# Swapping the rows for the turning by position with small transfers, in a fused float32 kernel on one Trainium2 core

## The chip, the core and the metric

The program runs on one core of a Trainium2 chip. The core has five engines that run side by side, each in its own written order, and that wait for each other through semaphores: TensorE (PE in the profile; its weight loads are shown as PEld), VectorE (DVE), ScalarE (ACT), GpSimd (POOL) and SyncE (SP, which here only issues transfers). The metric is the device time of one execution in microseconds, and less is better. The kernel before takes 1328.01 us, the median of three runs (1327.96 to 1329.7).

## The reference, cut to what matters

Two transformer blocks are computed in float32 for 256 tokens of width 1024. The change lies in the first of them, in what follows its wide input projection `w_in`:

```python
proj = xn @ w_in                       # (256, 1024) @ (1024, 4680)
u_pool, q, k, v, iq, ik, iw, gates = split(proj)
q, k, iq, ik = rope_partial(each)      # the turning by position

def rope_partial(x, pos):              # heads of 64; only the first 16 of each turn
    xr = x[..., :16]; x1, x2 = xr[..., :8], xr[..., 8:]
    rot = concatenate([x1 * cos - x2 * sin, x2 * cos + x1 * sin])
    return concatenate([rot, x[..., 16:]])

score = sum over 8 index heads of  iw * relu(iq @ ik / 8)   # then the 64 largest of a row
p     = softmax of q @ k / 8 over the kept keys;  o = p @ v
```

So a turned value needs the value that stands 8 rows away in its head. The kernel keeps activations with the channel on the partition and the token along the row, and two heads of 64 fill 128 partitions. The partner of partition 0 is therefore partition 8: another partition, which a vector engine does not reach.

## The kernel before, in words

Everything is a row of matrix products with 128-column chunks of weights. A weight matrix comes from memory in units of 128 partitions by 1024 numbers (512 KB, eight blocks of 128x128). SP loads each unit into one of nine buffers `raw` (L479), ACT rounds it into one of four buffers `whi` (L1137), DVE computes the rest `wlo` (L1595), and TensorE makes three products per block: high weight by high input (L558), high by low (L570), low by high (L572). The weight loads wait for nothing but the release of their buffer: the load of unit i waits until TensorE is done with unit i-9 (semaphore `mm`). Between the units of `w_in` stand the units called `ada`, two after every second unit from chunk 7 on (L663).

For `w_in` a unit is one output chunk: 38 chunks, numbered n, of 24 products each. In what follows "chunk n" is that one. The functions `tensor_program`, `vector_program`, `scalar_program`, `gpsimd_program` and `sync_program` write out each engine's order by walking over the same chunks, and tables say what stands after which chunk. The steps around the change are:

- Once chunk n is done, DVE scales it (`rescaled_in`, L1622). Thirteen chunks, in the list `ROPE` (0 to 4 and 6 to 13), hold channels that turn. The first four are the index queries, the fifth the index key, then q and k.
- Three chunks later TensorE multiplies the scaled chunk by a permutation matrix with signs (`during_in`, L830), DVE multiplies this by the sines (L1809), and POOL multiplies the chunk by the cosines (L2307) and adds the two (L2310). The semaphore `rope` counts finished turnings.
- `INDEX_MM`: after chunks 8 to 15 TensorE makes the products of one pair of index heads each (L777, jobs 0 to 7; jobs 0 to 3 have 128 columns, jobs 4 to 7 have 256), ACT takes them through the relu (L1184), and DVE adds them up one chunk later (`INDEX_SUM`, L1726 and L1729).
- `INDEX_LARGEST`: after chunks 16 to 24 DVE looks for the largest scores in rounds of eight (L1745, L1747).
- After chunks 25, 27, 29 and 31 come the attention scores of two heads each (L789), DVE takes the maximum, ACT the exponential (L1192), DVE the inverse of the sums (L1775), POOL the probabilities (L2296), and from chunk 27 on TensorE turns these to the other side (`turned1`, L798).
- After chunks 17 to 20 the v chunks are turned to token rows (L843), copied by ACT (`vtok`, L1240).
- The split for later units is put between these steps: DVE makes the low half of chunk c+3 after the work that follows chunk c, and ACT makes the high half at about the same place.
- `seqs` and the context `ctx`, which the second block alone needs, are loaded among the units of `w_in` (L495, L497).

Of the kernel before, what the change touches and what calls it, by code (L numbers as in the profile page):

```python
# [20 lines left out]
CONSTS = {}  # L21
# [45 lines left out]

INDEX_MM = {8 + i: i for i in range(8)}
INDEX_SUM = {u + 1: job for u, job in INDEX_MM.items()}
# [219 lines left out]
def launch_program(nc, dram, out):  # L289
# [81 lines left out]
    def h32(name, cols, at):  # L371
        return sb(name, cols, at=h_at + at)
# [14 lines left out]
    mask = h32("mask", 384, 52736)  # L387
    wtok = h32("wtok", 2 * 128, 58880).rearrange("p (b c) -> p b c", b=2)
    branch = h32("branch", 2048, 0).rearrange("p (c t) -> p c t", c=8)
# [72 lines left out]


    def sync_program(e):
        w = Waits(e)

        def load(i):
# [25 lines left out]
        for i in range(NRAW, len(PLAN)):  # L493
            if i == 24:
                e.dma_start(R[:, :, 256:512], dram["ctx"]).then_inc(S("ctx").sem, 16)  # L495
            if i == 44:
                e.dma_start(seqs, dram["seqs"]).then_inc(S("seqs").sem, 16)  # L497
            load(i)
            if PLAN[i] == ("na_in", 5):
                for h in range(4):  # L500
                    load_bias(h)

            at = i - (NRAW - 1)
            if at > 0 and PLAN[at][0] == "na_in":
                _, scores, _ = attend2(PLAN[at][1])
                if scores and scores[1] == 1 and scores[0] < 6:
                    for x in range(2):
                        load_bias(2 * scores[0] + 4 + x)
# [6 lines left out]
    def tensor_program(e):  # L515
# [301 lines left out]
        def during_in(n):  # L817
# [6 lines left out]
            m = n - 3  # L824
            if m in ROPE:
                j = ROPE.index(m)
                w.wait_ge(S("resc_w_in"), m + 1)
                w.wait_ge(S("con"), 16)
                free6()
                e.matmul(ps[6][:, :256], const("perm"), tmp[j % 4][:, :256], start=True, stop=True).then_inc(S("rope_mm").sem, 1)  # L830
                bank6[0] = ("rope_s", j + 1)
            if m == 5:
                w.wait_ge(S("resc_w_in"), m + 1)
                free6()
                for b in range(2):
                    t = e.transpose(ps[6][:, 128 * b:128 * b + 128], iw[:, 128 * b:128 * b + 128], ident)
                t.then_inc(S("w_tr").sem, 1)
                bank6[0] = ("wtok", 1)
# [288 lines left out]
    def scalar_program(e):  # L1127
# [81 lines left out]
        for what, i in walk("w_in"):  # L1209
# [15 lines left out]
            if what == "chunk":  # L1225
# [16 lines left out]
                if i >= 22:  # L1242
                    w.wait_ge(S("resc_w_in"), i + 1)
                    e.activation(sig[:, i - 22], tmp[i % 4][:, :256], ACT.Tanh, scale=0.5).then_inc(S("sig").sem, 1)
                for g in POOLED_AT.get(i, ()):
# [340 lines left out]
    def vector_program(e):  # L1586
# [107 lines left out]
        def rescaled_in(n):  # L1694

            if n in ROPE:
                j = ROPE.index(n)
                if j >= 4:
                    w.wait_ge(S("rope"), j - 3)
                into = tmp[j % 4][:, :256]  # L1700
            elif n == 5:
                into = iw
            elif n < 18:
                into = vT[:, n - 14]
            elif n < 22:
                into = upad[:, n - 18, 16:272]
            else:
                if n < 26:
                    w.wait_ge(S("rope"), 13)
                else:  # L1710
                    w.wait_ge(S("sig"), n - 25)
                into = tmp[n % 4][:, :256]
            rescaled("n0", "w_in", n, rst[:, LEFT], into)
# [67 lines left out]
        for what, i in walk("w_in"):  # L1781
# [15 lines left out]
            if what == "chunk":  # L1797
                if i == 1:
                    mean_inverse("n0", rst[:, LEFT], ps[4][:, :256])
                    rescaled_in(0)  # L1800
                if i:
                    rescaled_in(i)
                if i - 3 in ROPE:
                    j = ROPE.index(i - 3)
                    w.wait_ge(S("rope_mm"), j + 1)
                    w.wait_ge(S("con"), 16)
                    if j >= 2:
                        w.wait_ge(S("rope"), j - 1)
                    e.tensor_tensor(X[j % 2][:, :256], ps[6][:, :256], const("rope_s"), MUL).then_inc(S("rope_s").sem, 1)  # L1809
                written("w_in", i)  # L1810
# [431 lines left out]
    def gpsimd_program(e):  # L2242
# [22 lines left out]
        for v in range(2):  # L2265
            e.memset(pick[:, v, v:v + 1], 1.0).then_inc(S("pick").sem, 1)
        e.memset(upad[:, :, 0:16], 0.0).then_inc(own.sem, own.up())
        e.memset(ptmp[:, :, 0:16], 0.0).then_inc(own.sem, own.up())
# [29 lines left out]
        for what, i in walk("w_in"):  # L2298
            if what == "unit" and i - 1 in SCORES:
                probabilities1(SCORES[i - 1])  # L2300
            if what == "chunk":
                if i - 3 in ROPE:
                    j = ROPE.index(i - 3)
                    x = tmp[j % 4][:, :256]
                    w.wait_ge(S("rope_mm"), j + 1)
                    w.wait_ge(S("con"), 16)
                    e.tensor_tensor(x, x, const("rope_c"), MUL).then_inc(own.sem, own.up())  # L2307
                    w.wait_ge(own, own.n)
                    w.wait_ge(S("rope_s"), j + 1)
                    e.tensor_tensor(rope_into[j], x, X[j % 2][:, :256], ADD).then_inc(S("rope").sem, 1)  # L2310
                if 18 <= i < 22:
# [247 lines left out]
```

## Time and profile before

| | |
|---|---|
| median of three runs | 1328.01 us |
| the profiled execution | 1328.15 us, span 1326.3 us |
| PE busy | 1311.0 us, 99% of the span |
| DVE busy | 827.1 us, 62% |
| ACT busy | 595.1 us, 45% |
| POOL busy | 416.8 us, 31% |
| granted TensorE clock | 1.00 over the span |

The busy share of PE says that it almost never lacks work; it doesn't say how long it would take if another engine were slower. For that one reads, stretch by stretch, how late the other engines deliver. In a timeline row the first two numbers are start and duration in us, then come engine, line, operation, what is written and read, the shapes and the count, and in brackets how long the engine had been idle and who ended that. Products overlap in the pipeline: 24 of them with 256 columns start 0.12 us apart although each is shown as 0.28 us.

### The profile page before, as it was taken

What the parts mean: (1) busy time and instruction counts of PE and PEld (TensorE: products, weight loads), DVE (VectorE), ACT (ScalarE), POOL (GpSimd) and SP (SyncE); (2) the same over time, 40 slices, a digit from 0 to 9 for tenths busy, and PEclk for the clock granted to TensorE, in tenths of its full rate; (3) what the DMA queues carried; (4) which work ended last, traced back from release to release, by engine and by line L of the source; (5) the groups of instructions that cost most, each with busy time, mean ns of one, the idle gap of its engine ahead of it and who ended that gap; (6) DMA issues with size and microseconds to landing.
All of it is one profiled execution on the core that took longest, in us unless ns stands there. A gap on an engine that the chain in (4) does not pass through costs nothing.

```text
span 1326.3 us, 19991 instructions
## 1 busy us (share of the span) xinstructions
PE 1311.0 (99%) x7852; PEld 1109.0 (84%) x7852; DVE 827.1 (62%) x1270; ACT 595.1 (45%) x953; POOL 416.8 (31%) x424
## 2 busy tenths in 40 slices
PE   9999999999999999999999999999999999999999
PEld 8788888999986788878788888787777777999987
DVE  6688578899876444388534444343667765855553
ACT  5336546566654133254311233222545543766432
POOL 2353222222411001245400144111366552488200
PEclk9999999999999999999999999999999999999999
DMA  7777457855555322254444444434623320555552
GB/s 294 257 279 248 151 194 277 291 177 189 181 185 177 125 96 80 96 206 159 159 141 145 143 143 143 143 143 153 228 64 112 111 81 32 207 185 182 191 190 80
DMA packets 63964, 220.08 MB, mean 166 GB/s; under 512 B 6912, under 2 KB 10240, under 8 KB 63872
## 3 DMA queue, kind: packets, MB, share of 16 engines
q1 hardware_dynamic: 63584, 218.56, 47.4%
q8 instruction: 63, 1.03, 0.3%
q10 hardware_dynamic: 288, 0.25, 0.1%
q14 instruction: 29, 0.24, 0.1%
HBM read 217.73 MB, written 1.05 MB: 165 GB/s over the span
## 4 chain that ended last, share of the span: by engine, by line
PE 91%; DVE 6%; issue 1%; ACT 1%; DMA 1%; POOL 0%; SPq 0%; DVEq 0%; ACTq 0%
PE ps L558 23%; PE ps L570 22%; PE ps L572 22%; PE ps L548 8%; PE ps L550 4%; PE ps L663 2%; PE ps L1000 1%; DVE wlo L1595 1%; PE ps L1027 1%; PE ps L1014 1%; DVE xn L2054 1%; PE ps L993 1%; DVE A L2046 1%; PE ps L608 1%; DMA R<-in_x 1%
## 5 line engine op out<-in xcount | busy, mean ns | idle before, releaser
L558 PE MATMUL ps<-A,whi 128*128 128x256 f32 (+2 forms) x1580 | 519.2, 329 | 1.5 <-DVE A L1827 0.8
L572 PE MATMUL ps<-A,wlo 128*128 128x256 f32 (+2 forms) x1552 | 495.9, 320 | 0.2 <-DVE wlo L1595 0.2
L570 PE MATMUL ps<-A,whi 128*128 128x256 f32 (+2 forms) x1552 | 495.8, 319 | 0.2 <-DVE A L1608 0.2
L1595 DVE TENSOR_TENSOR wlo<-raw,whi 128x1024 fp32r<-128x1024 f32 x305 | 390.3, 1283 | 92.4 <-ACT whi L1137 92.1
L1137 ACT ACTIVATE whi<-raw 128x1024 fp32r<-128x1024 f32 x305 | 319.9, 1051 | 280.7 <-PE ps L572 162.4
L558 PEld LDWEIGHTS ps<-A,whi 128*128 128x128 f32 x1580 | 299.9, 190 | 52.7 <-issue 23.7
L570 PEld LDWEIGHTS ps<-A,whi 128*128 128x128 f32 x1552 | 295.2, 190 | 22.1 <-issue 1.7
L572 PEld LDWEIGHTS ps<-A,wlo 128*128 128x128 f32 x1552 | 294.6, 190 | 21.4 <-DVE wlo L1595 0.4
L2248 POOL TENSOR_TENSOR H<-tmp,H 128x256 fp32r<-128x256 f32 (+1 forms) x86 | 123.5, 1436 | 62.2 <-ACT H L1430 42.6
L548 PE MATMUL ps<-H,whi 128*128 128x512 f32 x400 | 140.2, 397 | 0.0
L550 PE MATMUL ps<-H,wlo 128*128 128x256 f32 x400 | 111.7, 279 | 0.0
L2364 POOL TENSOR_TENSOR tmp<-tmp 128x512 f32<-128x512 f32 (+1 forms) x64 | 57.6, 900 | 159.0 <-ACT tmp L1425 159.0
L572 PE MATMUL ps<-H,wlo 128*128 128x512 f32 (+1 forms) x280 | 106.7, 381 | 0.6 <-DVE wlo L1595 0.6
L558 PE MATMUL ps<-H,whi 128*128 128x512 f32 (+1 forms) x280 | 107.0, 382 | 0.0
L570 PE MATMUL ps<-H,whi 128*128 128x512 f32 (+1 forms) x280 | 106.5, 380 | 0.0
L2019 DVE SCALAR_TENSOR_TENSOR R<-ps,ada,R 128x256 f32<-128x256 f32 x56 | 24.8, 479 | 114.6 <-PE ps L572 113.4
L548 PEld LDWEIGHTS ps<-H,whi 128*128 128x128 f32 x400 | 75.2, 188 | 17.9
L2259 POOL TENSOR_TENSOR ssum<-ssum,sq 128x256 f32<-128x256 f32 (+1 forms) x30 | 32.0, 1067 | 172.3 <-ACT sq L1152 172.3
L550 PEld LDWEIGHTS ps<-H,wlo 128*128 128x128 f32 x400 | 75.4, 189 | 0.0
L1673 DVE SCALAR_TENSOR_TENSOR modsum<-raw,cond,modsum 128x1024 f32<-128x1024 f32 x36 | 63.3, 1776 | 0.0
L558 PEld LDWEIGHTS ps<-H,whi 128*128 128x128 f32 x280 | 52.7, 188 | 11.6 <-issue 0.8
L572 PEld LDWEIGHTS ps<-H,wlo 128*128 128x128 f32 x280 | 52.7, 188 | 10.9 <-DVE wlo L1595 0.8
(297 smaller groups left out, 1477.0 us busy)
## 6 DMA issues: line engine op xcount, KB each, us to landing
raw<-in_ada SPq DMA_DIRECT2D x96, 512.0 KB, 4.3
raw<-in_w SPq DMA_DIRECT2D x64, 512.0 KB, 3.5
raw<-in_w_up SPq DMA_DIRECT2D x44, 512.0 KB, 4.4
raw<-in_w_in SPq DMA_DIRECT2D x38, 512.0 KB, 5.5
raw<-in_w_0a SPq DMA_DIRECT2D x32, 512.0 KB, 3.6
raw<-in_w_0b SPq DMA_DIRECT2D x32, 512.0 KB, 3.5
raw<-in_na_in SPq DMA_DIRECT2D x24, 512.0 KB, 6.4
raw<-in_w_down SPq DMA_DIRECT2D x22, 512.0 KB, 4.3
```

Of the source, the lines that this page charges most:

```text
L548: e.matmul(bank, w_hi, both(k), start=k == 0, stop=False)
L550: m = e.matmul(o, w_lo, ah, start=False, stop=last)
L558: e.matmul(o, w_hi, ah, start=k == 0, stop=False)
L570: e.matmul(o, w_hi, al, start=False, stop=False)
L572: m = e.matmul(o, w_lo, ah, start=False, stop=last)
L663: m = e.matmul(ps[7][q:q + 32, :], cond[:, k, :], raw[slot][:, 512 * j:512 * j + 512], start=k == 0 or i in (88, 89), stop=k == 7 and i < 48)
L1137: e.activation(whi[s % NHI][:, :cols], raw[i % NRAW][:, :cols], ACT.Copy).then_inc(S("whi").sem, 1)
L1595: e.tensor_tensor(wlo[i % NRAW][:, :cols], raw[i % NRAW][:, :cols], plain(whi[s % NHI][:, :cols]), SUB).then_inc(S("wlo").sem, 1)
L1673: d = e.scalar_tensor_tensor(total, raw[i % NRAW], cond[:, k, v:v + 1], total, MUL, ADD)
L2248: e.tensor_tensor(into, x, plain(hi), SUB).then_inc(S(done).sem, 1)
L2259: e.tensor_tensor(total, total, x, ADD).then_inc(S(st + "_part").sem, 1)
L2364: e.tensor_tensor(x, x, x, MUL).then_inc(S(st + "_sq").sem, 1)
```

## The change

The 13 products with the permutation are gone. The scaled chunks are kept in 13 tiles `turning`, and in three groups (chunks 0 to 4, 6 to 9, 10 to 13) their rows are swapped by four transfers each, from `turning` to `swapped`: 8 rows of up to 1280 numbers go 8 partitions up or down, for both heads. SP issues them between the weight loads, and waits there for the scaled chunks and, for the second and third group, until the turnings of the group before are done and `swapped` is free. The sign is put once into the sine table by POOL. DVE multiplies the swapped rows by the sines in place, now a row read from SBUF and not from PSUM. When the turnings of a chunk are done is set by the table `TURN_AT`: they come in twos and threes and later than before. The index products stand after chunks 12 to 19 (before: 8 to 15), their sums after chunks 13 to 20. The context and `seqs` are loaded among the units of `w_up`.

```diff
-INDEX_MM = {8 + i: i for i in range(8)}
+INDEX_MM = {12 + i: i for i in range(8)}
...
+    turning = h32("turning", 13 * 256, 22528)
+    swapped = h32("swapped", 5 * 256, 54272)
...
+    GROUPS = (range(5), range(5, 9), range(9, 13))
+    TURN_AT = {9: (0, 1, 2), 10: (3, 4), 14: (5, 6), 15: (7, 8), 18: (9, 10), 19: (11, 12)}
...
+        def swap(x):
+
+            g = GROUPS[x]
+            w.wait_ge(S("resc_w_in"), ROPE[g[-1]] + 1)
+            if x:
+                w.wait_ge(S("rope"), g[0])
+            else:
+                w.wait_ge(S("swapped0"), 1)
+            cols = 256 * len(g)
+            for at in (0, 64):
+                for into, of in ((at, at + 8), (at + 8, at)):
+                    e.dma_start(swapped[into:into + 8, :cols],
+                                turning[of:of + 8, 256 * g[0]:256 * g[0] + cols]).then_inc(S(f"swap{x}").sem, 16)
...
         for i in range(NRAW, len(PLAN)):
-            if i == 24:
+            for x, g in enumerate(GROUPS):
+                if PLAN[i - NRAW] == ("w_in", ROPE[g[-1]] + 2):
+                    swap(x)
+            if PLAN[i] == ("w_up", 4):
                 e.dma_start(R[:, :, 256:512], dram["ctx"]).then_inc(S("ctx").sem, 16)
-            if i == 44:
+            if PLAN[i] == ("w_up", 12):
                 e.dma_start(seqs, dram["seqs"]).then_inc(S("seqs").sem, 16)
...
-            if m in ROPE:
-                j = ROPE.index(m)
+            if m == 5:
                 w.wait_ge(S("resc_w_in"), m + 1)
                 w.wait_ge(S("con"), 16)
-                free6()
-                e.matmul(ps[6][:, :256], const("perm"), tmp[j % 4][:, :256], start=True, stop=True).then_inc(S("rope_mm").sem, 1)
-                bank6[0] = ("rope_s", j + 1)
...
                 if i >= 22:
                     w.wait_ge(S("resc_w_in"), i + 1)
+                    w.wait_ge(S("rope"), 13)
...
-                if i - 3 in ROPE:
-                    j = ROPE.index(i - 3)
-                    w.wait_ge(S("rope_mm"), j + 1)
-                    w.wait_ge(S("con"), 16)
-                    if j >= 2:
-                        w.wait_ge(S("rope"), j - 1)
-                    e.tensor_tensor(X[j % 2][:, :256], ps[6][:, :256], const("rope_s"), MUL).then_inc(S("rope_s").sem, 1)
+                for j in TURN_AT.get(i, ()):
+                    w.wait_ge(S(f"swap{[j in g for g in GROUPS].index(True)}"), 64)
+                    w.wait_ge(S("rope_sign"), 2)
+                    r = swapped_of(j)
+                    e.tensor_tensor(r, r, const("rope_s"), MUL).then_inc(S("rope_s").sem, 1)
...
+        e.memset(swapped, 0.0).then_inc(S("swapped0").sem, 1)
+        w.wait_ge(S("con"), 16)
+        w.wait_ge(S("swapped0"), 1)
+        for h in range(2):
+            s = con[64 * h:64 * h + 8, CONSTS["rope_s"][0]:CONSTS["rope_s"][0] + 256]
+            e.tensor_scalar(s, s, -1.0, 1.0, MUL, MUL).then_inc(S("rope_sign").sem, 1)
...
-                    e.tensor_tensor(rope_into[j], x, X[j % 2][:, :256], ADD).then_inc(S("rope").sem, 1)
+                    e.tensor_tensor(rope_into[j], x, swapped_of(j), ADD).then_inc(S("rope").sem, 1)
```

SP's queue before, where the loads that follow the release by chunk 14 stand. `raw` is a weight buffer with its number; a row without brackets waits for nothing.

```order
L479 DMA raw3_52<-in_w_in 128x1024 [waits s_mm]
L479 DMA raw4_53<-in_w_in 128x1024 [waits s_mm]
L479 DMA raw5_54<-in_ada 128x1024 [waits s_mm]
L479 DMA raw6_55<-in_ada 128x1024 [waits s_mm]
L479 DMA raw7_56<-in_w_in 128x1024 [waits s_mm]
L479 DMA raw8_57<-in_w_in 128x1024 [waits s_mm]
```

The same place now, where the third group stands in it.

```order
L508 DMA raw3_52<-in_w_in 128x1024 [waits s_mm]
L508 DMA raw4_53<-in_w_in 128x1024 [waits s_mm]
L493 DMA swapped_123<-turning_122 8x1024 [waits s_rope,s_rescaled]
L493 DMA swapped_123<-turning_122 8x1024 x3
L508 DMA raw5_54<-in_ada 128x1024 [waits s_mm]
L508 DMA raw6_55<-in_ada 128x1024 [waits s_mm]
L508 DMA raw7_56<-in_w_in 128x1024 [waits s_mm]
L508 DMA raw8_57<-in_w_in 128x1024 [waits s_mm]
```

Four loads stand behind the wait for `rope`: two `ada` units (raw5, raw6) and the units of chunks 20 (raw7) and 21 (raw8). The two in front of it are chunks 18 and 19. The second group stands in the same way ahead of two `ada` units and chunks 16 and 17.

DVE before, from the low half of chunk 20 (raw7) to that of chunk 21 (raw8). `upad` is the scaled chunk 18, `score` the sums of the index heads.

```order
L1595 TENSOR_TENSOR wlo7_65<-raw7_56,whi0_67 128x1024 [waits s_whi]
L1622 TENSOR_TENSOR upad_117<-ps0,rst_104 128x256 [waits s_mm]
L1745 MAX small_84<-score_118 128x8 [waits s_v_step]
L1747 MATCH_REPLACE score_118<-small_84,score_118 128x128 [waits s_v_step]
L1745 MAX small_84<-score_118 128x8 [waits s_v_step]
L1747 MATCH_REPLACE score_118<-small_84,score_118 128x128 [waits s_v_step]
L1595 TENSOR_TENSOR wlo8_66<-raw8_57,whi1_68 128x1024 [waits s_whi]
```

DVE now, between the same two low halves.

```order
L1622 TENSOR_TENSOR wlo7_65<-raw7_56,whi0_67 128x1024 [waits s_whi]
L1649 TENSOR_TENSOR upad_117<-ps0,rst_104 128x256 [waits s_mm]
L1829 TENSOR_TENSOR swapped_123<-swapped_123,con_75 128x256 [waits s_swap2]
L1829 TENSOR_TENSOR swapped_123<-swapped_123,con_75 128x256
L1751 SCALAR_TENSOR_TENSOR score_120<-Y0_100,wtok_124,score_120 128x256 [waits s_idx_acc,s_idx_relu]
L1751 SCALAR_TENSOR_TENSOR score_120<-Y1_101,wtok_124,score_120 128x256 [waits s_idx_acc,s_idx_relu]
L1767 MAX small_84<-score_120 128x8 [waits s_v_step]
L1769 MATCH_REPLACE score_120<-small_84,score_120 128x128 [waits s_v_step]
L1767 MAX small_84<-score_120 128x8 [waits s_v_step]
L1769 MATCH_REPLACE score_120<-small_84,score_120 128x128 [waits s_v_step]
L1622 TENSOR_TENSOR wlo8_66<-raw8_57,whi1_68 128x1024 [waits s_whi]
```

Two products by the sines and one pair of index sums have come in between.

## Rows read from the trace of the kernel before

**Rows 1.** Waits of TensorE from 10 to 130 us: total us, times, longest.

```profile
engine line waited for: us in total, times, longest us
PE ps L558 <- DVE tmp L1622: 0.6, 1, 0.6
```

**Rows 2.** Timeline of TensorE at 77 us, then at 50 us.

```profile
76.81 0.28 PE L572 MATMUL ps<-A,wlo 128*128 128x256 f32 x1
76.93 0.59 PE L830 MATMUL ps<-tmp,con 128*128 128x256 f32 x2
...
77.48 0.28 PE L570 MATMUL ps<-A,whi 128*128 128x256 f32 x1
...
50.12 0.49 PE L777 MATMUL ps<-ik,iq 64*128 64x128 f32 x4
50.54 0.39 PE L558 MATMUL ps<-A,whi 128*128 128x256 f32 x1
```

**Rows 3.** Busy time by stretch: PE, PEld, DVE, ACT, POOL (x instructions), clock, DMA share, GB/s.

```profile
42.00:80.00 38.00, 38.00 (x291) 30.59 (x291) 26.10 (x42) 13.10 (x25) 11.94 (x16) 1.00 0.78 275
...
92.00:115.00 23.00, 23.00 (x190) 19.76 (x189) 21.46 (x52) 11.05 (x19) 10.60 (x15) 1.00 0.89 322
...
200.00:250.00 50.00, 50.00 (x381) 42.73 (x380) 42.33 (x67) 29.78 (x47) 11.26 (x14) 1.00 0.82 284
```

**Rows 4.** Timeline of DVE, chunk 14 to chunk 25.

```profile
67.87 0.42 DVE L1622 TENSOR_TENSOR vT<-ps,rst 128x256 f32<-128x256 f32 x1 [1.70 <-PE ps L572]
...
71.99 0.42 DVE L1622 TENSOR_TENSOR vT<-ps,rst 128x256 f32<-128x256 f32 x1 [0.62 <-PE ps L572]
...
77.13 0.42 DVE L1622 TENSOR_TENSOR vT<-ps,rst 128x256 f32<-128x256 f32 x1 [1.64 <-PE ps L572]
77.56 0.42 DVE L1809 TENSOR_TENSOR X<-ps,con 128x256 f32<-128x256 f32 x1
77.90 1.62 DVE L1729 SCALAR_TENSOR_TENSOR score<-Y,wtok,score 128x256 f32<-128x256 f32 x2
...
80.35 1.22 DVE L1595 TENSOR_TENSOR wlo<-raw,whi 128x1024 fp32r<-128x1024 f32 x1
81.49 0.42 DVE L1622 TENSOR_TENSOR vT<-ps,rst 128x256 f32<-128x256 f32 x1
81.82 0.29 DVE L1745 MAX8 small<-score 128x8 f32<-128x128 f32 x1
...
83.13 1.22 DVE L1595 TENSOR_TENSOR wlo<-raw,whi 128x1024 fp32r<-128x1024 f32 x1
84.71 0.42 DVE L1622 TENSOR_TENSOR upad<-ps,rst 128x256 f32<-128x256 f32 x1 [0.37 <-PE ps L572]
...
87.81 0.42 DVE L1622 TENSOR_TENSOR upad<-ps,rst 128x256 f32<-128x256 f32 x1 [0.23 <-PE ps L572]
...
92.09 0.42 DVE L1622 TENSOR_TENSOR upad<-ps,rst 128x256 f32<-128x256 f32 x1 [1.16 <-PE ps L572]
...
110.30 0.42 DVE L1622 TENSOR_TENSOR tmp<-ps,rst 128x256 f32<-128x256 f32 x1
```

**Rows 5.** Timeline of POOL: the adding of a turning, under a low half and clear of one.

```profile
24.79 1.60 POOL L2310 TENSOR_TENSOR iq<-tmp,X 128x256 f32<-128x256 f32 x1
...
45.36 0.75 POOL L2307 TENSOR_TENSOR tmp<-tmp,con 128x256 f32<-128x256 f32 x1 [5.79 <-PE ps L830]
```

**Rows 6.** Line L479, 20 to 130 us: SP's time per load (ns), and issue to landing.

```profile
L479 SPq DMA_DIRECT2D raw<-in_w_in x29: 327/328/432, 19.7 to 122.1; - x29
...
DMA to landing us min/median/max: 2.5/4.8/6.6
```

**Rows 7.** Timeline of ACT at 80 us: high half of chunk 20, then the v chunk.

```profile
79.04 1.06 ACT L1137 ACTIVATE whi<-raw 128x1024 fp32r<-128x1024 f32 x1 [4.38 <-DMA raw<-in_w_in]
80.64 0.38 ACT L1240 ACTIVATE vtok<-ps 128x256 f32<-128x256 f32 x1 [0.55 <-PE ps L843]
```

**Rows 8.** Timelines of POOL and TensorE: head 0's probabilities, and their turning after chunk 27.

```profile
115.15 0.48 POOL L2296 TENSOR_SCALAR Y<-X,small 128x256 f32<-128x256 f32 x1
...
116.67 0.49 PE L798 MATMUL ps<-con,Y 128*128 128x128 f32 x3
```

More of the change, by code:

```diff
@@ L387, in launch_program @@
     mask = h32("mask", 384, 52736)
-    wtok = h32("wtok", 2 * 128, 58880).rearrange("p (b c) -> p b c", b=2)
+    turning = h32("turning", 13 * 256, 22528)
+    swapped = h32("swapped", 5 * 256, 54272)
+    wtok = h32("wtok", 2 * 128, 59392).rearrange("p (b c) -> p b c", b=2)
     branch = h32("branch", 2048, 0).rearrange("p (c t) -> p c t", c=8)
@@ L461, in launch_program, with turning_of, swapped_of @@
                 turn2["scores", 4 * p + 2 * b + x] = len(turn2)
+    GROUPS = (range(5), range(5, 9), range(9, 13))
+    TURN_AT = {9: (0, 1, 2), 10: (3, 4), 14: (5, 6), 15: (7, 8), 18: (9, 10), 19: (11, 12)}
+    def turning_of(j):
+        return turning[:, 256 * j:256 * j + 256]
+    def swapped_of(j):
+        at = 256 * [j - g[0] for g in GROUPS if j in g][0]
+        return swapped[:, at:at + 256]
     def sync_program(e):
         w = Waits(e)
+        def swap(x):
[10 more added lines that the diff above has]
+                                turning[of:of + 8, 256 * g[0]:256 * g[0] + cols]).then_inc(S(f"swap{x}").sem, 16)
         def load(i):
@@ L824, in during_in @@
             m = n - 3
-            if m in ROPE:
-                j = ROPE.index(m)
+            if m == 5:
                 w.wait_ge(S("resc_w_in"), m + 1)
                 w.wait_ge(S("con"), 16)
-                free6()
-                e.matmul(ps[6][:, :256], const("perm"), tmp[j % 4][:, :256], start=True, stop=True).then_inc(S("rope_mm").sem, 1)
-                bank6[0] = ("rope_s", j + 1)
-            if m == 5:
-                w.wait_ge(S("resc_w_in"), m + 1)
                 free6()
@@ L1696, in rescaled_in @@
             if n in ROPE:
[L1697 to L1700, printed above, removed]
+                into = turning_of(ROPE.index(n))
             elif n == 5:
@@ L1707, in rescaled_in @@
             else:
-                if n < 26:
-                    w.wait_ge(S("rope"), 13)
-                else:
+                if n >= 26:
                     w.wait_ge(S("sig"), n - 25)
@@ L2266, in gpsimd_program @@
             e.memset(pick[:, v, v:v + 1], 1.0).then_inc(S("pick").sem, 1)
+        e.memset(swapped, 0.0).then_inc(S("swapped0").sem, 1)
[4 more added lines that the diff above has]
+            e.tensor_scalar(s, s, -1.0, 1.0, MUL, MUL).then_inc(S("rope_sign").sem, 1)
+            w.wait_ge(S("rope_sign"), h + 1)
         e.memset(upad[:, :, 0:16], 0.0).then_inc(own.sem, own.up())
@@ L2301, in gpsimd_program @@
             if what == "chunk":
[L2302 to L2305, printed above, removed]
+                for j in TURN_AT.get(i, ()):
+                    x = turning_of(j)
+                    w.wait_ge(S(f"swap{[j in g for g in GROUPS].index(True)}"), 64)
                     w.wait_ge(S("con"), 16)
```

## The prediction

> **What bounds the kernel now.** I read the page first: PE is busy 99% of the span, so time can only be saved by giving TensorE less to do, and only where nobody makes it wait instead. Next the waits of TensorE over the input projection: a single one of 0.6 us [rows 1]. Here its own instruction stream is the bound. Then the busy time by stretch [rows 3]: from 42 to 80 us DVE works 26.1 of 38 us, but from 92 to 115 us 21.46 of 23 us. There it is the second bound, right behind. So I went through DVE's timeline from chunk 16 to chunk 25 [rows 4]. Its idle time there is 0.37, 0.23 and 1.16 us, 1.8 in all, the last of it at 92.09; after that it waits for nobody until chunk 25 is scaled at 110.30. Last I looked at what follows chunk 25, for the place where DVE's lateness reaches TensorE. The probabilities of head 0 are ready at 115.15 + 0.48 = 115.63, and TensorE turns them at 116.67 [rows 8]. TensorE has 1.04 us to spare there, and no more.
>
> **What is removed.** 13 products with the permutation. One starts at 76.93; the L572 before it started at 76.81, the L570 two places on at 77.48 [rows 2]. That is 0.67 us where the 0.12 us rhythm would give 0.24, so one costs 0.43 us and 13 cost 5.6 us, all of it on TensorE. This is the most that the change can bring.
>
> **Index products four chunks later.** The sum on TensorE is the same: 0.42 us for a job of 128 columns from 50.12 to 50.54 in [rows 2], and I estimate twice that, 0.84, for 256. But until chunk 16 they make TensorE run further ahead. New ends of chunks, from the starts of the scaling in [rows 4]: chunk 14 at 67.87 - 10 x 0.43 - 2.5 = 61.1, chunk 15 at 71.99 - 4.7 - 2.9 = 64.4, chunk 16 at 77.13 - 5.2 - 3.4 = 68.5, chunk 17 some 3.7 later at 72.2, chunk 18 at 84.71 - 5.6 - 1.7 = 77.4. Unhindered, TensorE would be at the turning after chunk 27 at 116.67 - 5.6 = 111.1.
>
> **DVE's work moves into its full stretch.** From the low half of chunk 20 (83.13) to the scaling of chunk 25 (110.30) are 27.2 us, 25.4 without the 1.8 idle [rows 4]. Three pairs of index sums now stand in it that were done before: 1.62 us shown per pair, 1.55 with the overlap, 4.65 in all. So do four products by the sines, each 0.34 from start to start (77.56 to 77.90), 1.4 in all. The stretch becomes 25.4 + 4.65 + 1.4 = 31.4 us. When can it start? Chunk 14: scaling 0.33 (81.49 to 81.82), two sine products 0.7, a pair of sums 1.4, low half 1.14 (80.35 to 81.49), so from 61.1 to 64.7. Chunk 15 the same, to 68.3: just in time for chunk 16 at 68.5. Chunk 16 took 3.2 us up to its low half (77.13 to 80.35) and now has no sine product, 2.9, then the low half: 72.5. Chunk 17: scaling, a pair, two rounds of the search (81.82 to 83.13, 1.3), 3.2 in all: DVE could start at 75.7. With this alone chunk 25 is scaled at 75.7 + 31.4 = 107.1, 3.2 us earlier than before and not 5.6.
>
> The sine product used to read PSUM and now reads SBUF twice. In this trace a POOL addition takes 1.60 us when it begins under a low half, and 0.75 is normal for POOL's product of the same size [rows 5]; a low half has two SBUF inputs too. The Trainium skill, "SBUF — State Buffer", section "Terms", says that DVE and GpSimd take turns at a shared port pair, that one holds it for the whole instruction and the other blocks. The trace agrees with its 0.85 us. By that rule the 13 sine products would now also block, which before they did not, 13 x 0.34 = 4.4 us at most, most of it in gaps. The sum here stays with the rows.
>
> **The swaps in SP's queue.** SP issues in order and takes 0.33 us each [rows 6], so a group takes 1.3. Group 0 has nine chunks' time before its turnings. Group 2 waits until nine turnings are done. DVE gives the first of the four that are missing at 61.1 + 0.7 = 61.8, and POOL then has seven operations of 0.82 (0.75 and the gap), to 67.6 at the earliest; each low half in their way costs 0.85, and with two of them it is 69.3, which I take. Behind this wait stand two `ada` loads and the loads of chunks 20 and 21. Before, they went out with the buffers' release, 64.4 for the first. Now the third, chunk 20's, starts at 69.3 + 1.3 + 0.7 = 71.3. A load lands after 4.8 us (median), at most 6.6 [rows 6]; as the third of a burst I give it 5.7: 77.0. Then ACT's high half of 1.06 [rows 7] is done at 78.1, and DVE, which wanted it at 75.7, stands still for 2.4 us. ACT's copy of the v chunk and the relus of the index job come behind that same high half, at 78.5 to 79.3, while TensorE asks for them at 77.4: a stop of 1 to 2 us, which costs nothing of its own if TensorE is stopped later anyway. Group 1 is similar and smaller: the loads of chunks 16 and 17 leave some 3 us late, but the context's 1 MB no longer runs ahead of them.
>
> What the small transfers themselves take no row shows. The lower bound is nothing, since they carry 8 rows; the upper one per transfer is the shortest landing here, 2.5 us, of a 256 KB load [rows 6]. I take no delay beyond the issue for the loads behind, because their rings hold only some KB for them, and keep the upper end for the range. The Trainium skill, "DMA: Bandwidth & Descriptors", section "Why a DMA increments its semaphore by 16 and not by 1", says that a transfer is shared by the largest number of engines up to 16 that divides its slowest dimension: here 8. No row here shows that.
>
> **The sum.** Chunk 25 is scaled at 78.1 + 31.4 = 109.5, that is 0.8 us earlier than 110.30. Scores, exponentials, inverses and probabilities follow as before, so head 0 is ready at 115.63 - 0.8 = 114.8, TensorE goes on there and not at 111.1, and is 1.04 + 0.8 = 1.8 us ahead of before. From there on each step is released by TensorE itself and the 1.8 stays. The other edits count as nothing. POOL's clearing and sign steps stand before 24 us, where it has nothing to do. TensorE's first index job (after chunk 12) needs five turnings. By the same prices POOL has nine operations for them from some 18 us before chunk 14's end, where chunk 9's first sine product is done, and ends them after 9 x 0.82 + 2 x 0.85 = 9.1 us, near 52; chunk 12 ends two chunks of 2.9, two jobs and an `ada` pair of 1.1 before 61.1, near 53.4. Without that cover the stop is the lateness, up to 2 us, and the one at chunk 27 swallows it. The wait for 13 turnings ahead of chunk 22's gate is met some 5 us early. The context and `seqs`, 1.6 MB, go where transfers are busy 0.82 of the time against 0.78 [rows 3]; they delay the loads of w_up by 2 to 4 us, and the cover is the lead of the nine buffers, which keeps TensorE busy for all 50 us of that stretch at a DMA share of 0.82. If the cover failed it would cost up to 4 us.
>
> The profiled execution took 1328.15, 0.14 more than the median. 1328.01 - 1.8 = 1326.2.
>
> **Rivals.**
> 1. *The loads are not late, only DVE's own work counts.* POOL's chain ends at 67.6, or the loads land in under 4 us. Then chunk 25 is scaled at 107.1, and the gain is 1.04 + 3.2 = 4.2: 1323.8. For it speaks that DVE's sum has few unknowns; against it, that the wait for nine turnings stands ahead of the loads whatever the rest does.
> 2. *DVE keeps up.* If its steps have slack that I don't see (sums inside what I count as busy), all of the 5.6 stays: 1322.4. Against it stand 21.46 us of 23.
> 3. *The small transfers hold up the weights (slower).* Place: SP's queue and rings behind group 2. Each us that chunk 20 lands later than 77.0 goes through high half, low half, DVE's full stretch and the probabilities to TensorE, one for one. From 78.8 on nothing is gained, from then on the kernel is slower. With half the upper bound for each of four transfers, 4 x 1.25 = 5 us, it is 1331.2. The worst landing of a common load, 6.6, alone brings 0.9 of it.
> 4. *Nothing moves.* The 1.8 is lost in one more landing of the slow kind: 1328.0. It differs from my forecast by size alone.
>
> **How the numbers follow.** Chances: my forecast 0.42, rival 1 0.20, rival 2 0.12, rival 3 0.15, rival 4 0.11. A measurement here can tell about 0.2%, 2.7 us, from no change. Faster by that are rivals 1 and 2 and the good end of my own case: 0.37. Slower is most of rival 3: 0.15. Within: 0.48. The range: 1322.4 if all of the 5.6 stays, and up to 1330.4, which takes in the lateness of landings and half of rival 3's.
>
> **What would show it.** No L830; chunk 16 scaled near 68.5 (row of DVE). SP without an issue from about 61 to 69, then four small transfers and a burst of loads. ACT's high half of chunk 20 ended near 78 and released by a DMA, with DVE idle before its low half and TensorE idle 1 to 2 us after chunk 18. DVE without idle time from there to chunk 25 at about 109.5. TensorE stopped for 2 to 3 us ahead of its first turning of probabilities, near 115. I am wrong if TensorE passes chunk 27 near 111 without a stop; if the loads behind group 2 leave by 67; or if TensorE stops at the first index job or in w_up.

## The result, and the profile after

| | median us (range) | ratio to before, 95% interval | profiled execution, span | clock |
|---|---|---|---|---|
| before, same comparison | 1329.26 (1327.92 to 1331.28) | | 1328.15, 1326.3 | 1.000 |
| changed kernel | 1333.88 (1331.64 to 1337.07) | 1.0036 [1.0028, 1.0044] | 1333.93, 1332.1 | 0.996 |

The change makes the kernel slower, by 0.36%. I had forecast 1326.2 us in a range up to 1330.4: wrong in sign and outside the range.

TensorE's waits from 60 to 90 us, where before it had none [rows 1]:

```profile
PE ps L869 <- ACT vtok L1266: 3.8, 1, 3.8
PE ps L809 <- ACT Y L1210: 2.0, 1, 2.0
```

They stand after chunk 14 (from 61.5 us) and after chunk 18 (from 81.9). Both name ScalarE, but its timeline shows what it waited for itself: each time a high half that waits for its load.

```profile
62.27 1.06 ACT L1163 ACTIVATE whi<-raw 128x1024 fp32r<-128x1024 f32 x1 [7.80 <-DMA raw<-in_w_in]
63.23 0.43 ACT L1210 ACTIVATE Y<-ps 128x128 f32<-128x128 f32 x2
...
84.26 1.06 ACT L1163 ACTIVATE whi<-raw 128x1024 fp32r<-128x1024 f32 x1 [9.69 <-DMA raw<-in_w_in]
85.22 0.37 ACT L1266 ACTIVATE vtok<-ps 128x256 f32<-128x256 f32 x1
```

In [rows 7] the high half of chunk 20 waited 4.38 us and made nobody late; here it waits 9.69, and the copy of the v chunk and the relus stand behind it in ScalarE's queue. Why the loads are late is to be read in SyncE's queue (start, time, number of transfers):

```profile
46.66 0.33 SPq L508 DMA_DIRECT2D raw<-in_w_in  x1
53.43 2.65 SPq L493 DMA_DIRECT2D swapped<-turning  x4
56.13 0.91 SPq L508 DMA_DIRECT2D raw<-in_ada  x2
57.09 0.91 SPq L508 DMA_DIRECT2D raw<-in_w_in  x2
...
59.24 2.64 SPq L508 DMA_DIRECT2D raw<-in_w_in  x2
73.40 2.65 SPq L493 DMA_DIRECT2D swapped<-turning  x4
76.10 0.91 SPq L508 DMA_DIRECT2D raw<-in_ada  x2
77.06 0.90 SPq L508 DMA_DIRECT2D raw<-in_w_in  x2
```

From 47.0 to 53.4 and from 61.9 to 73.4 SyncE issues nothing: it stands at the wait for five and for nine turnings. Part of that costs nothing, since the loads behind it are due only when chunks 11 and 15 end, at 49.5 and 68.8. Then come four small transfers, 2.65 us together, and behind them the loads of chunks 16 (57.09) and 20 (77.06) in bursts of seven. One small transfer takes 0.62 to 0.80 us of SyncE (line L493, ns: shortest, median, longest), a load 0.33 [rows 6]. The loads from 50 to 90 us land after 7.6 us in the median, against 4.8 before [rows 6]:

```profile
L493 SPq DMA_DIRECT2D swapped<-turning x12: 624/628/795, 30.1 to 75.4; - x12
...
DMA to landing us min/median/max: 3.5/7.6/10.1
```

What VectorE (first fence) and GpSimd (second) did of it: the low halves of chunks 16 and 20, the scaling of chunk 25, and the end of the ninth turning at 71.53 + 1.80 = 73.3.

```profile
63.36 1.23 DVE L1622 TENSOR_TENSOR wlo<-raw,whi 128x1024 fp32r<-128x1024 f32 x1 [5.21 <-ACT whi L1163]
...
85.35 1.22 DVE L1622 TENSOR_TENSOR wlo<-raw,whi 128x1024 fp32r<-128x1024 f32 x1 [5.77 <-ACT whi L1163]
...
116.18 0.42 DVE L1649 TENSOR_TENSOR tmp<-ps,rst 128x256 f32<-128x256 f32 x1
```

```profile
51.76 1.60 POOL L2337 TENSOR_TENSOR ik<-turning,swapped 128x256 f32<-128x256 f32 x1
...
71.53 1.80 POOL L2337 TENSOR_TENSOR qT<-turning,swapped 128x256 f32<-128x256 f32 x1
```

In [rows 4] chunk 25 was scaled at 110.30, now at 116.18. The stretches around the two stops (columns as in [rows 3]):

```profile
60.00:64.00 4.00, 1.98 (x17) 1.78 (x15) 0.64 (x1) 1.39 (x3) 0.00 (x0) 1.00 1.02 393
64.00:66.00 2.00, 2.00 (x15) 1.88 (x14) 2.00 (x5) 1.39 (x3) 0.61 (x1) 0.78 1.03 418
66.00:70.00 4.00, 4.00 (x26) 3.02 (x25) 3.29 (x6) 1.84 (x4) 3.50 (x5) 0.69 0.52 210
...
82.00:86.00 4.00, 0.36 (x2) 0.29 (x2) 0.65 (x1) 1.74 (x4) 0.00 (x0) 0.95 1.02 412
86.00:88.00 2.00, 2.00 (x8) 1.09 (x7) 2.00 (x5) 1.84 (x5) 0.62 (x1) 0.50 1.00 410
88.00:90.00 2.00, 2.00 (x15) 2.00 (x14) 1.83 (x6) 0.85 (x2) 1.92 (x4) 0.75 0.24 96
```

After each stop TensorE's granted clock is low (0.50 from 86 to 88 us, which is 1.2 of 2.4 GHz) and then comes back to 1.00. Each stop costs TensorE more than its length. Chunk 15 ends 7.24 us after chunk 14 and chunk 19 9.38 us after chunk 18; in e2_groups_later below, with the same work and no stop, it is 3.48 and 3.91. That is 3.76 and 5.47 us for stops of 2.02 and 3.78, 1.7 us more each time. The clock rows account for it: 0.22 of 2 us and 0.31 of 4 us are missing behind the first stop, 1.7 together, and 0.50 and 0.25 of 2 us behind the second, 1.5, with 0.05 of 4 us before that.

### The profile page after: what moved, and what is told of

Same layout as the page of the kernel before. It is cut to its first block, busy times and chain, and to the rows that moved or that the text cites. A ratio compares the mean times of both kernels' runs of the same rounds, so it can differ in the third digit from the quotient of the medians.

```text
span 1332.1 us, 19946 instructions
## 1 busy us (share of the span) xinstructions
PE 1311.5 (98%) x7826; PEld 1108.7 (83%) x7826; DVE 830.2 (62%) x1270; ACT 594.8 (45%) x953; POOL 425.0 (32%) x427
## 4 chain that ended last, share of the span: by engine, by line
PE 87%; DVE 7%; ACT 2%; issue 2%; DMA 1%; POOL 0%; SPq 0%; DVEq 0%; ACTq 0%; POOLq 0%
PE ps L590 22%; PE ps L602 21%; PE ps L604 21%; PE ps L580 8%; PE ps L582 4%; DVE wlo L1622 1%; PE ps L1026 1%; PE ps L695 1%; PE ps L1053 1%; ACT A L1188 1%; PE ps L1040 1%; DMA raw<-in_w_in 1%; PE ps L1019 1%; DVE A L2066 1%; DMA R<-in_x 1%
## 5 line engine op out<-in xcount | busy, mean ns | idle before, releaser
L1622 DVE TENSOR_TENSOR wlo<-raw,whi 128x1024 fp32r<-128x1024 f32 x305 | 394.7, 1298 | 104.0 <-ACT whi L1163 103.5
```

Source lines behind the costliest of these rows:

```text
L1622: e.tensor_tensor(wlo[i % NRAW][:, :cols], raw[i % NRAW][:, :cols], plain(whi[s % NHI][:, :cols]), SUB).then_inc(S("wlo").sem, 1)
```

## The experiments

**Whose wait, which queue.** Theories Q (the weights stand behind SyncE's wait), S (the small transfers themselves hold them up), D (VectorE's full stretch). e1_own_tile gives every swapped chunk its own place, so that no wait for turnings is left; place and number of the transfers are the same.

```diff
-    swapped = h32("swapped", 5 * 256, 54272)
+    swapped = sb("swapped", 13 * 256, at=a_at)
...
-            if x:
-                w.wait_ge(S("rope"), g[0])
-            else:
-                w.wait_ge(S("swapped0"), 1)
+            w.wait_ge(S("swapped0"), 1)
```

> The changed kernel with a tile of its own for the swapped rows of all 13 chunks (13 KB, where the high inputs of the next stage come later), so that groups 1 and 2 need not wait until the turnings of the group before are done. The twelve transfers, their places in SP's queue and all else stay. Theory Q (the weight loads stand behind a wait for turnings in SP's queue): the loads behind the groups leave at the release of their buffers plus 2.6 us of issuing, TensorE loses its stops of 2.0 us (relus after chunk 14) and 3.8 us (v copy after chunk 18) and its lowered clock; ratio to before 0.9965 to 0.9985, about 6 to 8 us under the changed kernel. Rival S (the small transfers themselves hold up the weights on the rings): the loads behind them still land 7 us after issue and the ratio stays above 1.002. Rival D (DVE's full stretch is what costs): the stops of TensorE move to the probabilities at chunk 27 and the ratio is 1.000 to 1.002.

e2_groups_later keeps the wait, and issues groups 1 and 2 two chunks later:

```diff
-                if PLAN[i - NRAW] == ("w_in", ROPE[g[-1]] + 2):
+                if PLAN[i - NRAW] == ("w_in", ROPE[g[-1]] + (4 if x else 2)):
```

> The changed kernel with groups 1 and 2 of the swaps two chunks later in SP's queue: the two ada loads and two chunk loads that stood behind the wait for turnings now stand ahead of it. The tile and the wait stay. Theory Q: the same gain as with a tile of its own, ratio 0.9965 to 0.9985, since the turnings that are waited for end near 53 and 66 us while the queue arrives there near 54 and 69. Rival S: as many stops as in the changed kernel, ratio above 1.002. Rival D: 1.000 to 1.002.

Measured: e1 1325.51, ratio 0.9974 [0.9963, 0.9986]; e2 1324.92, 0.9970 [0.9959, 0.9981] (before in the same comparison 1329.44). Both stops are gone in both profiled executions, and the clock is 1.000. Q holds. S falls with e1, where all 12 transfers stand ahead of the same loads as in the changed kernel, take the same 2.65 us of SyncE, and hold up nobody. e1's queue:

```profile
46.85 2.65 SPq L490 DMA_DIRECT2D swapped<-turning  x4
...
50.73 3.02 SPq L505 DMA_DIRECT2D raw<-in_w_in  x2
...
61.75 2.65 SPq L490 DMA_DIRECT2D swapped<-turning  x4
```

e2's queue, its VectorE, and TensorE's wait of that stretch:

```profile
50.91 3.02 SPq L508 DMA_DIRECT2D raw<-in_w_in  x2
54.04 2.65 SPq L493 DMA_DIRECT2D swapped<-turning  x4
...
66.83 3.03 SPq L508 DMA_DIRECT2D raw<-in_w_in  x2
70.33 2.65 SPq L493 DMA_DIRECT2D swapped<-turning  x4
```

```profile
75.74 1.22 DVE L1622 TENSOR_TENSOR wlo<-raw,whi 128x1024 fp32r<-128x1024 f32 x1
78.15 0.42 DVE L1649 TENSOR_TENSOR upad<-ps,rst 128x256 f32<-128x256 f32 x1 [1.19 <-PE ps L604]
...
107.84 0.42 DVE L1649 TENSOR_TENSOR tmp<-ps,rst 128x256 f32<-128x256 f32 x1
```

```profile
PE ps L830 <- POOL Y L2324: 1.5, 1, 1.5
```

TensorE is 5.1 us ahead of before at chunk 27 and then stops for 1.5 before the first turning of probabilities: 3.4 remain at chunk 28. That is D's share.

**The other parts alone, in the kernel before.** e3_index_later has `INDEX_MM = {12 + i: i ...}`, e4_context_in_w_up the two late loads.

> The kernel before with one edit: the index products after chunks 12 to 19 and their sums after 13 to 20. Three pairs of sums (4.65 us) come into DVE's full stretch, and TensorE comes 3.4 us earlier to chunk 16. My step on DVE says chunk 25 is scaled near 111.3, 1.0 us later than before, just what TensorE had to spare: ratio 0.9995 to 1.0010. Rival D: DVE's stretch alone makes the kernel slower by 2 us or more, 1.0015 to 1.003.

> The kernel before with one edit: the context and seqs loaded in w_up at the new places. All theories that put the loss in w_in: 0.9995 to 1.0005, no new wait of TensorE in w_up. Rival C (the loads of w_up come late behind the 1.6 MB): 1.001 to 1.003, with TensorE waiting for low halves between 205 and 260 us.

Measured: e3 1329.75, ratio 1.0001 [0.9991, 1.001]; e4 1328.0, 0.9997 [0.9988, 1.0006]. Neither changes the time by what can be measured, and TensorE has no wait from 200 to 260 us in e4. The trace of e3 still shows the price of the later index sums: chunk 25 is scaled at 112.91, where I expected 111.3, TensorE stops once, and chunk 28 ends at 123.8, 1.7 us later than before.

```profile
PE ps L798 <- POOL Y L2296: 0.5, 1, 0.5
```

**Each group by itself.** e6_only_group1_later and e7_only_group2_later are the changed kernel with `(4 if x == 1 else 2)` and `(4 if x == 2 else 2)`.

> The changed kernel with group 1's transfers alone two units later. Theory B (each group's wait costs by itself): the stop after chunk 14 is gone (3 us), group 2's wait stays: SyncE reaches it at 65.0, waits for the nine turnings to 70.3, its transfers go until 72.9, chunk 20's load is issued near 74 and lands 80 to 81.2, and TensorE stops 3 to 4.5 us after chunk 18, with 1.5 us of lowered clock behind; VectorE's stretch at chunk 27 gives 1.5 back. Time 1327.5 to 1330, best guess 1329. Rival O (group 2 is late only because group 1 was): with group 1 in time no stop after chunk 18 over 0.5 us, time 1325 to 1325.8 as e2.

> The changed kernel with group 2's transfers alone two units later. Theory B: group 1's stop after chunk 14 stays (2 to 3 us and the lowered clock, 3.1 together), the one after chunk 18 is gone (its load no longer stands behind a wait: issued near 70.6, landed near 76.5), VectorE's stretch takes what it takes in e2 but with less: 1325.5 to 1327, best guess 1326.3. Rival O (all of the loss hangs on group 1's lateness): the stop after chunk 18 comes all the same, 3 us or more, 1330 or more.

Measured: e6 1328.72, ratio 0.9999 [0.9989, 1.001]; e7 1330.27, 1.0003 [0.9994, 1.0011]. Each group's wait costs by itself (theory B), and rival O falls: e6 still stops after chunk 18 with group 1 in time. The time of e7 would fit O too (1330 or more), but the stop after chunk 18 that O asks for is not there. Group 2 in its old place costs 3.8 us over e2 (1328.72 - 1324.92), group 1 5.4; together 9.2, and the changed kernel is 9.0 over e2. I had given group 1 only 1.4 (1326.3), and e7 missed its range. e7's twelve executions lie between 1327.26 and 1332.38, at mean clocks from 1.000 to 0.997, and e6's between 1327.91 and 1333.17, so which group is the dearer is not shown. Waits of TensorE from 60 to 90 us, e6 and then e7, with e7's stretch after the stop (its profiled execution took 1331.07):

```profile
PE ps L869 <- ACT vtok L1266: 2.7, 1, 2.7
```

```profile
PE ps L809 <- ACT Y L1210: 4.0, 1, 4.0
```

```profile
66.00:68.00 2.00, 2.00 (x11) 1.78 (x9) 2.00 (x5) 0.87 (x3) 0.68 (x1) 0.50 1.01 412
68.00:72.00 4.00, 4.00 (x27) 3.65 (x29) 2.60 (x5) 1.21 (x2) 3.34 (x4) 0.66 0.11 42
```

e7 stops for 4.0 us where the changed kernel stopped for 2.0, and e6 for 2.7 where I expected 3 to 4.5. Chunk 15 ends 9.91 us after chunk 14 in e7, 2.4 more than the stop and the 3.48 of e2; e6 loses 1.9 in the same way behind its own. e7's load of chunk 16 was issued at 57.12, as there at 57.09, and landed at 64.18, not 62.25. Why a burst of equal loads lands up to 2 us apart between two executions stays open.

**What a small transfer takes of SyncE.** e8_price_of_issue adds ten transfers that nobody reads:

```diff
+        SIZES = {16: (8, 256, con), 20: (8, 1024, con), 24: (8, 1024, dram["consts"]), 28: (128, 256, con), 32: (128, 1024, con)}
...
+                for x in range(2):
+                    e.dma_start(scratch[:rows, 1024 * x:1024 * x + cols], of[:rows, :cols]).then_inc(S(f"dummy{i}").sem, 16)
```

> The kernel before with the context loaded in w_up, and besides ten transfers that nobody reads, two each at five places of w_in, into a tile of their own: 8 rows of 256 elements from SBUF, 8 rows of 1024 from SBUF, 8 rows of 1024 from memory, 128 rows of 256 from SBUF, 128 rows of 1024 from SBUF. What SyncE takes to issue one: theory R (few rows make it dear) 0.62 to 0.80 us for the three of 8 rows, 0.33 for the two of 128; theory F (a source in SBUF makes it dear) 0.33 for the one from memory, 0.62 to 0.80 for the other four; theory W (it was dear in the changed kernel only because the waiting queue was full or two cover each other) 0.33 for all. The time is not asked: 1328 to 1331.

Its five pairs, in that order (a single execution, 1329.24 us):

```profile
33.91 1.52 SPq L504 DMA_DIRECT2D scratch<-con  x2
...
41.64 1.32 SPq L504 DMA_DIRECT2D scratch<-con  x2
...
50.26 0.66 SPq L504 DMA_DIRECT2D scratch<-in_consts  x2
...
59.09 1.19 SPq L504 DMA_DIRECT2D scratch<-con  x2
...
68.34 1.11 SPq L504 DMA_DIRECT2D scratch<-con  x2
```

Theory F holds: it is the source in SBUF that makes it dear, 0.56 to 0.76 us each at any size (I had expected 0.62 to 0.80), while 8 rows from memory take 0.33 like a load. Size and rows matter little. The Trainium skill, "DMA: Bandwidth & Descriptors", section "Why a DMA increments its semaphore by 16 and not by 1", says that where fewer than 16 engines share a transfer the issuing sequencer writes the rest of the 16 itself; eight rows would give eight engines. If those writes took time that shows, few rows would be dear. The third and fourth pair speak against that as the cause: 8 rows from memory are cheap, 128 rows from SBUF are not.

**The queue, tried once more.** e11_swapped_by_gpsimd leaves groups 1 and 2 at their old time and moves them, waits and all, from SyncE to GpSimd, behind the turning that frees the tile:

```diff
                     e.tensor_tensor(rope_into[j], x, swapped_of(j), ADD).then_inc(S("rope").sem, 1)
+                if i in (10, 15):
+                    swap(e, w, 1 if i == 10 else 2)
```

> The changed kernel, but groups 1 and 2 issued by GpSimd right behind the turning that frees the tile (the order and the waits for the turnings are kept; they stand in no queue of weights any more). Theory Q (the loss comes from the weight loads that stand behind SyncE's wait): no stop after chunks 14 and 18, SyncE issues chunk 16's load near 51 and chunk 20's near 67, and the time is as e2's or under it, 1324 to 1325.5. Rival L (the transfers come late in any case and VectorE's and GpSimd's turning work waits for them): group 1 is issued near 52.5, group 2 near 70, so the multiplications at chunks 14 and 18 find them landed; only if a transfer from GpSimd's queue takes over 7 us to issue and land does VectorE stop, with 1 to 3 us lost, 1326 to 1328.

```profile
54.04 2.27 POOL L490 DMA_DIRECT2D swapped<-turning  x4 [0.64 <-DVE turning L1648]
...
70.80 2.09 POOL L490 DMA_DIRECT2D swapped<-turning  x4 [0.56 <-POOL qT L2336]
```

Measured: 1325.34, ratio 0.9974 [0.9964, 0.9985], no stop after chunk 14 or 18. The transfers go out as SyncE's did (54.04 for 53.43 in the changed kernel, 70.80 for 70.33 in e2) and with the same waits. What matters is who queues behind them. Q is shown from a second side.

**What is left: VectorE's stretch.** Theory D2: its end sets chunk 27's stop. Each of the next four is e2 with one thing more changed: e10 leaves out two rounds (`23: [(1, 2)]` is taken from `INDEX_LARGEST`), e9 moves two, e5 moves the sums, e12 moves four products to GpSimd.

> e2_groups_later without the two rounds of the eight largest that stand at chunk 23 (the second block gets six rounds of eight; left out to take 1.75 us of VectorE out of the full stretch). Theory D2: the mask comes 1.7 us earlier, the stop of 1.5 us at chunk 27 is gone, the time is 1.5 to 1.7 us under e2's: 1323.3 us. Rival P: the stop stays over 1 us, the time within 0.4 of e2's.

Measured: 1323.63, ratio 0.9962 [0.9949, 0.9974]. Chunk 25 is scaled 2.0 us earlier than in e2, TensorE does not stop at chunk 27, and the span is 1320.8 against 1322.8. D2 holds, by the trace: the intervals of the two ratios overlap, [0.9949, 0.9974] and e2's [0.9959, 0.9981].

```profile
105.84 0.42 DVE L1649 TENSOR_TENSOR tmp<-ps,rst 128x256 f32<-128x256 f32 x1
```

Where TensorE stops at that place, chunk 28 ends 10.86 us after chunk 25 is scaled (10.85 in e9, e11 and e12; ends of chunks are good to 0.02 us). In e10, where TensorE arrives just as the probabilities are ready, it is 10.87:

| | chunk 25 scaled | chunk 28 ends | difference |
|---|---|---|---|
| before (does not stop) | 110.30 | 122.09 | 11.79 |
| changed kernel | 116.18 | 127.04 | 10.86 |
| e7 | 114.22 | 125.08 | 10.86 |
| e6 | 111.26 | 122.12 | 10.86 |
| e2 | 107.84 | 118.70 | 10.86 |

The 0.93 between 11.79 and 10.86 is what TensorE had to spare before (1.04 by [rows 8]).

> e2_groups_later with two of the rounds of the eight largest of the first block moved from chunks 19 and 20 to chunks 17 and 18 (and its mask left at 20). VectorE stood 1.2 us before chunk 18 in e2. Theory D2 (the end of VectorE's full stretch sets chunk 27's stop): the rounds fill that gap, the rest of the stretch and the mask come 1.2 us earlier (105.3 us, not 106.5), the stop of 1.5 us at chunk 27 shrinks to 0.3, and the time is 1.2 us under e2's: 1323.7 us. Rival P (the stop belongs to the chain of ScalarE and GpSimd behind it, or VectorE has slack elsewhere): the stop stays at 1.5 us and the time at 1324.9.

e9: `17: [(0, 3)], 18: [(0, 3)], 19: [(0, 1)]`. Measured 1324.98, 0.9975 [0.9965, 0.9984]; the stop is 1.4. My reckoning was off: only one of the two rounds comes before the gap, and a pair of sine products met GpSimd's work and took 1.51 us for e2's 0.77. The number is the one rival P gave, a stop of 1.5 and 1324.9. It tells nothing against D2 all the same, since chunk 25 is scaled only 0.26 us earlier than in e2 (107.58) and chunk 28's end follows it by the same 10.85. Nothing is gained.

```profile
84.23 1.51 DVE L1829 TENSOR_TENSOR swapped<-swapped,con 128x256 f32<-128x256 f32 x2
```

> Groups 1 and 2 two units later, as in e2_groups_later, and besides group 0 turned at chunks 8 and 9 (not 9 and 10), the index's heads from chunk 11 (not 12). Theory D2 (what e2 still loses at chunk 27, 1.7 us of 5.1, is VectorE's full stretch from 78 to 110 us, whose end lets the mask, the scores and chunk 27's turning go): one index sum of 1.84 us leaves the stretch, the mask comes 1.8 us earlier, the stop of 1.5 us at chunk 27 is gone or under 0.3, and the time is 1.3 to 1.7 us under e2's: 1323.4 us. Rival P (the stop is the ScalarE and GpSimd chain of the probabilities itself, or the earlier first index job makes TensorE wait for the five turnings, which end near 49.4 when chunk 11 ends at 49.5): the stop stays at 1.5 us, or another of 0.5 to 1 us comes after chunk 11, and the time is 1324.5 to 1325.5.

e5: `INDEX_MM = {11 + i: i ...}` and `TURN_AT = {8: (0, 1, 2), 9: (3, 4), ...}`. Measured 1325.47, 0.9972 [0.9961, 0.9983]: nothing gained, a new stop of 0.9 us at the first index product (for `ik` from GpSimd), 1.2 left at chunk 27. Rival P had foreseen such a stop after chunk 11 and 1324.5 to 1325.5. Inconclusive for D2, since TensorE itself was 1.5 us later from chunk 12 on.

> e2_groups_later, but the four products by the sines of group 2 are made by GpSimd, which then adds them. Theory D2 (chunk 28's end is chunk 25's scaling + 10.86 us, and VectorE is without idle time from 78 us to there): 1.37 us (78.49 to 79.16, 83.69 to 84.39) leave the stretch, chunk 25 is scaled at 106.5 and not 107.84, chunk 28 ends at 117.3 and the time is 1.3 us under e2's: 1323.6. Rival K (GpSimd's four more operations hold VectorE up by as much as they take from it, some 0.75 us for each that meets one of two SBUF inputs): chunk 25 is scaled at 107.8 or later and nothing is gained, 1325 to 1326.

```diff
+                    if j >= 9:
+                        continue
...
+                        e.tensor_tensor(swapped_of(j), swapped_of(j), const("rope_s"), MUL).then_inc(own.sem, own.up())
```

Measured 1324.74, 0.9965 [0.9952, 0.9979]; chunk 25 is scaled at 108.00 and the stop is 1.5 as in e2. Rival K holds, though the time lies just under its 1325 to 1326: 1.4 us of work left VectorE and nothing came of it. The pairs of index sums took 0.7 us less in all than in e2, but the seven low halves of this stretch took 1.4 more (up to 1.67 each for e2's 1.22), and VectorE now waited 0.4 for TensorE. The low half of 85.22 (chunk 22's) ran beside GpSimd's first product by the sines; in e2 it took 1.22:

```profile
85.22 1.57 DVE L1622 TENSOR_TENSOR wlo<-raw,whi 128x1024 fp32r<-128x1024 f32 x1
87.19 0.42 DVE L1649 TENSOR_TENSOR upad<-ps,rst 128x256 f32<-128x256 f32 x1 [0.40 <-PE ps L604]
```

```profile
85.66 1.72 POOL L2339 TENSOR_TENSOR swapped<-swapped,con 128x256 f32<-128x256 f32 x1
```

The Trainium skill, "SBUF — State Buffer", section "Terms", says that these two engines take turns at a shared port pair; the 0.35 us here and the 0.74 of e9 agree in kind.

e2 is the version to take: 1324.92, faster than both kernels. e1, e5, e9, e11 and e12 cannot be told from it.

## Why the prediction was wrong

- **What is removed** was right in its size. With the waits out of the way (e2) TensorE is 5.1 us ahead at chunk 27, the 5.6 less 0.5 in its first chunks.
- **Index products four chunks later** was right: chunk 14 ends at 61.5 for 61.1, five turnings at 51.76 + 1.60 = 53.4 for my 52, and chunk 12 ends at 53.6. TensorE does not stop at the first index product.
- **VectorE's full stretch** was right: from chunk 20's low half to chunk 25's scaling I had 31.4 us, the trace has 116.18 - 85.35 = 30.8. In e2, where the loads are in time, the low half starts at 75.74 (I had 75.7), the stretch takes 32.1, and the time, 1324.92, is near rival 1's, "loads are not late", 1323.8.
- **The step that failed** is "The swaps in SP's queue", at the sentence "Group 1 is similar and smaller: the loads of chunks 16 and 17 leave some 3 us late". It has no working, and nothing of it went into the sum: group 1 was put at no stop of TensorE and no delay of VectorE. The loads behind its wait are due when chunk 11 ends, 49.5, and the wait goes to 53.4. The prediction's own figures do give 3 us: turnings at 52, 1.3 for the four transfers, 0.7 for two loads, 54.0 in all, against 50.91 in e2. Measured, it is 6.2 (57.09 for 50.91): the turnings end 1.4 later than I had them, the four transfers take 1.35 more, the two loads ahead 0.3 more. With 3 us chunk 16 would have landed near 59.2 and its high half ended near 60.3, before chunk 14 did (an estimate from these rows), and TensorE would not have stopped there. With 6.2 it lands at 62.25: TensorE stops, VectorE stands for 5.2 us, and with it stand the very turnings for which group 2 waits: nine are done at 73.3, not at 69.3. e7, which keeps this part alone, is 5.4 us over e2.
- **Mis-sized beside it**: a group's issue, 2.65 us and not 1.3 (0.33 was a load's, from memory; e8), and the landing of the third load in a burst, 84.24 - 77.06 = 7.2 and not 5.7. Chunk 20 so lands at 84.24 instead of 77.0: 4.1 us from the turnings, 1.35 from the issue, 0.3 from the spacing of the loads, 1.5 from the landing.
- **Rival 3's line** (each us that chunk 20 lands later comes through one for one) was right in its slope: 7.2 us later, and the profiled execution is 1333.93 where my forecast for it was 1326.35. Its cause was not. I had it from what the transfers do to the rings, which e1 excludes. It needed the waits. The 6.7 us by which chunk 25 is scaled later than my 109.5 are these 7.2 less the 0.6 of the stretch.
- **"Costs nothing of its own"**, of the stop after chunk 18, held by a narrow margin. TensorE came to the turning 0.65 us before it could go on:

```profile
121.56 0.55 PE L830 MATMUL ps<-con,Y 128*128 128x128 f32 x3 [0.65 <-POOL Y L2324]
```

  The two stops and the 1.7 us of lowered clock behind each, 9.2 us together, had taken its lead of 5.1 and 4.1 more, and VectorE's lateness let it go on only 4.9 after before (121.56 for 116.67).
- **The products by the sines**, which now read SBUF twice, were left out of the sum with an upper bound of 4.4 us from 0.34 each. A pair clear of others takes 0.75 us (64.83); one took 1.70, so 0.34 was no bound for one product. Over all thirteen I count 1.7 us, none of it in the full stretch.

```profile
47.01 1.70 DVE L1829 TENSOR_TENSOR swapped<-swapped,con 128x256 f32<-128x256 f32 x2
```

- None of the prediction's three signs of being wrong appeared. It had not named a stop after chunk 14, which is where the loss begins.
- About 1 us of the 5.8 by which the span grew comes after 970 us, among the chunks of `na_in`, which the change does not touch. The granted clock from 960 to 1000 us is 0.96 there, and 1.00 before and in e2; why stays open.

## What to carry to other kernels

A wait put into a queue that also issues the loads delays every load behind it, so its price is worked out for each place where it stands, and in order of time: the first such place moves the releasers of the next. The same wait is free where nothing urgent queues behind it, two chunks later or on an engine that has to wait there anyway. Price an issue from a row with the same kind of source and destination, and where an engine is full to the last us, moving work away from it pays only if the engine that takes it over does not contend with it.

## What the hardware showed that I had not expected

- A transfer out of SBUF takes SyncE 0.56 to 0.76 us to issue, one out of memory 0.33, for 8 rows and for 128 alike (e8; the changed kernel 0.62 to 0.80). From GpSimd's queue four of them take 2.1 to 2.3 us.
- Each stop of 2.0 and 3.8 us cost TensorE 1.7 us more through its clock, which fell to 1.2 GHz after TensorE had stood and came back while it worked; the stops of 2.7 us in e6 and 4.0 us in e7 cost 1.9 and 2.4 more. Only part of this reached the kernel's time, since VectorE was later still.
- The same load, issued at 57.1 us as third in a burst of seven, landed at 62.25 in one kernel and at 64.18 in another.
